# Order of the attention units in the first layer: short units one by one between long ones

## The reference, cut to what matters

```python
k_all = concatenate([k_ctx, k_lat], axis=1)         # 256 context + 1024 latent tokens
v_all = concatenate([v_ctx, v_lat], axis=1)
o_lat = _attend(q_block, k_all, v_all)              # per block of 128 latent queries
if with_ctx_out:                                    # first layer only
    o_ctx = _attend(heads_q(bq_c), k_ctx, v_ctx)    # context queries see 256 keys

def _attend(q, k, v):
    s = einsum('bqkgd,bskd->bkgqs', q, k) * ATTN_SCALE
    p = softmax(s, axis=-1)
    return einsum('bkgqs,bskd->bqkgd', p, v)
```

## Time and profile before

| | us |
|---|---|
| median of 3 runs (4020.82 to 4025.8) | 4024.08 |
| profiled execution | 4020.44 |
| its span | 4018.6 |
| PE busy (share of the span) | 3839.8 (96%) |
| DVE busy | 1755.6 (44%) |
| ACT busy | 1408.8 (35%) |

### The profile page before, as it was taken

One profiled execution on the slowest core, in us unless ns is written; L12 is line 12 of the kernel. 1 busy time (PEld: TensorE's weight loads), 2 busy tenths in 40 slices (PEclk: granted clock), 3 DMA queues, 4 the chain that ended last, 5 costly groups with the idle time before them and its releaser, 6 DMA issues.

```text
span 4018.6 us, 44730 instructions
## 1 busy us (share of the span) xinstructions
PE 3839.8 (96%) x16064; PEld 2101.0 (52%) x16064; DVE 1755.6 (44%) x3695; ACT 1408.8 (35%) x3419; POOL 714.8 (18%) x904
## 2 busy tenths in 40 slices
PE   8999899999999899999999999999999999979995
PEld 3444466655444466655466666545666644433331
DVE  3543567345254466445365465202233311254445
ACT  3433556123233455224345444311233312121112
POOL 1021000032012000032043344102222100013331
PEclk9999899999999999999999999999999999989997
DMA  5101210022110232122101001101101110159997
GB/s 209 42 1 37 93 69 25 30 79 74 72 42 1 105 126 75 37 76 74 65 6 40 22 27 68 46 18 55 44 12 42 67 42 0 64 201 362 369 355 279
DMA packets 88744, 346.64 MB, mean 86 GB/s; under 512 B 21176, under 2 KB 53440, under 8 KB 69712
## 3 DMA queue, kind: packets, MB, share of 16 engines
q1 hardware_dynamic: 70096, 304.94, 20.4%
q0 software_dynamic: 18432, 38.85, 2.6%
HBM read 401.31 MB, written 37.83 MB: 109 GB/s over the span
## 4 chain that ended last, share of the span: by engine, by line
PE 89%; DVE 4%; ACT 2%; issue 2%; DMA 1%; SPq 0%; POOL 0%; DVEq 0%; POOLq 0%; ACTq 0%
PE psum L88 40%; PE psum L94 9%; PE psum L1609 6%; PE psum L3434 6%; PE psum L2065 5%; PE psum L947 4%; PE psum L924 4%; PE psum L3456 3%; PE psum L2315 3%; PE psum L2083 1%; PE psum L320 1%; PE psum L2272 1%; PE psum L1446 1%; DMA arena<-w_in 0%; PE psum L1996 0%
## 5 line engine op out<-in xcount | busy, mean ns | idle before, releaser
L88 PE MATMUL psum<-arena 128*128 128x512 f32 (+3 forms) x4416 | 1737.4, 551 | 13.7 <-DVEq L180 8.1
L88 PEld LDWEIGHTS psum<-arena 128*128 128x128 f32 x4416 | 832.6, 191 | 835.0 <-issue 774.5
L94 PE MATMUL psum<-arena 128*128 128x128 f32 (+2 forms) x3020 | 437.5, 278 | 25.8 <-DMA arena<-hn_scratch,arena 5.8
L94 PEld LDWEIGHTS psum<-arena 128*128 128x128 f32 (+2 forms) x3020 | 340.5, 141 | 225.5 <-issue 158.3
L2065 PE MATMUL psum<-arena 128*128 128x512 f32 (+1 forms) x640 | 285.4, 573 | 9.0 <-DVE arena L2116 4.8
L1609 PE MATMUL psum<-arena 128*128 128x512 f32 x576 | 259.8, 599 | 0.9 <-ACT arena L1733 0.9
L3434 PE MATMUL psum<-arena 128*64 x512 | 229.0, 601 | 7.4 <-issue 5.7
L3435 PE MATMUL psum<-arena 128*64 128x512 f32 x512 | 229.0, 601 | 0.0
L947 PE MATMUL psum<-arena 64*128 64x512 f32 (+1 forms) x800 | 167.7, 551 | 21.3 <-ACT arena L1037 13.4
L1037 ACT ACTIVATE arena<-psum,arena 128x1280 f32<-128x1280 f32 (+1 forms) x144 | 176.8, 1233 | 20.0 <-DVE arena L989 18.2
L175 DVE SCALAR_TENSOR_TENSOR arena<-psum,arena 128x512 f32<-128x512 f32 x62 | 42.7, 689 | 299.3 <-ACT arena L172 299.3
(11 more groups left out here) (415 smaller groups left out, 4935.2 us busy)
## 6 DMA issues: line engine op xcount, KB each, us to landing
arena<-w_gu SPq DMA_DIRECT2D x32, 2048.0 KB, 10.4
arena<-w_ada SPq DMA_DIRECT2D x24, 2048.0 KB, 8.0
arena<-w_dn SPq DMA_DIRECT2D x32, 1024.0 KB, 14.7
arena<-w_in SPq DMA_DIRECT2D x12, 2048.0 KB, 8.7
arena<-w_out SPq DMA_DIRECT2D x6, 2048.0 KB, 8.1
arena<-gate_rows_scratch SPq DMA_DIRECT2D x36, 256.0 KB, 3.5
x_scratch<-arena SPq DMA_DIRECT2D x18, 512.0 KB, 3.2
arena<-x SPq DMA_DIRECT2D x16, 512.0 KB, 9.4
```

What stands on the lines that cost most here:

```text
L88: ins = e.matmul(out, l, r, start=(i == 0), stop=(i == n - 1))
L94: ins = e.transpose(o, i, idn)
```

## The change

The order of the units of the first layer. The second layer has no short units, so its order stays. The functions of the engines are not touched: they read the order from `att_units`.

```diff
         def att_units(l):
-            return [(t, h) for t in tiles_of(l) for h in range(0, 8, 2)]
+            short = [(t, h) for t in tiles_of(l) for h in range(0, 8, 2) if t < NC_T]
+            long = [(t, h) for t in tiles_of(l) for h in range(0, 8, 2) if t >= NC_T]
+            n = len(short) + len(long)
+            return [short.pop(0) if u % 4 == 1 and short else long.pop(0) for u in range(n)]
```

## The result

The changed kernel takes 4032.95 us (median of 7 runs, 4028.57 to 4036.91), the kernel before 4020.82 in the same number of runs (4008.9 to 4025.8). The ratio is 1.0036, 95% interval 1.0026 to 1.0045: slower by 12 us in the medians and 14 by the ratio. The profiled execution took 4033.37 us, its span is 4031.6, against 4018.6.

A forecast was written before the change was run, and what follows sets the result against it. PE's own work was taken to bound the long part, with the chain from scores to next scores just under it. To 4020.4 us came 14.6 for the order and 5 for clock falls: 4040.0 us, range 4026 to 4060.

The forecast's parts named there:

- the clock term: In the stage's slots with idle: three falls of PE's clock, 5 us; bounds 0 to 27 us.
- slots D: Slots with all neighbours long: 7.66 us as before, all PE work.
- Slot A: Slot with the short unit's scores, transposes and values of two long ones: all work, 5.95 us.
- B: Slot with long scores, the short unit's transposes and a product: 1.79 us idle, 9.27 us long.
- C: Slot with long scores, the short unit's values and the turn: some 1.7 us idle, 7.84 us long.
- Both gates: After long scores: product or turn not before 7.41 us, behind ACT's copy; next scores not before a 7.11 us chain.
- The start 14.2 us: Stage's first two slots: slot 0, long with nothing beside it, 8.5 us; slot 1, 5.7 us.
- The sum, +14.6 us to the scores of unit 39: Stage up to unit 39's scores: 299.9 us against 285.35 before, without any effect of the clock.
- my two kinds of row: PE idle of 3.15 us, or 0.66 and 1.13 close together, preceded clock falls; gaps such as 0.65 us didn't.
- The rival of falls in most rounds: Clock falls twelve times or more in the stage: 35 us, 4055, up to 4062 with sixteen; chance 0.14.
- The rival on the faster side: Short units' waits hidden, rounds pure PE work of 27.2 us: 13.6 us less, 4006.8; chance 0.12.
- The rival of no change: Gates come about 0.9 us sooner in 16 slots beside short units, 14.6 us in all: 4020; chance 0.08.

The follow-up runs named there:

- early_copy: Changed kernel with ACT's copy of the values of unit u-2 moved ahead of one or both exponentials where possible; 4022.46 us, ratio to before 1.0010.
- short_at_3: Changed kernel with the short units moved to slots 3, 7, ..., 31, the slots of the turns; ratio to before 1.0035.
- half: Changed kernel with four short units first (0 to 3) and the other four at slots 5, 9, 13 and 17; ratio to before 1.0017.
- short_last: Changed kernel with all 32 long units first and the 8 short ones at the end; 4011.31 us, ratio to before 0.9984.
- one_first: Against the kernel with all short units last: one short unit first, then 32 long, then the other 7 short; ratio to before 0.9974.
- short_last_2: The same kernel with all 8 short units last, run on a second occasion; ratio to before 0.9972.

## Why the prediction was right, and where it was off

The direction, the mechanism and the range held (4032.95 in 4026 to 4060); the point, 4040.0, was 7 us high. Had the clock term been left out, the sum would have been 4035.0, 2 us from the measured median; that is in part luck, since the stage came out 0.8 us longer than its sum and the time outside it 2 to 3 us shorter. Its steps:

- *PE's own work bounds the long part.* Held: slots D are 7.66 us in every kernel.
- *Slot A 5.95, B 9.27, C 7.84, D 7.66.* Measured 5.94, 9.24, 7.97, 7.66; a round 30.81 instead of 30.72. C came out 0.13 us long, 1 us over eight rounds, and the mis-sized term is the turn. Its gate came at 7.38 us as forecast (7.41), opened by ACT's copy, but from there to the next scores it took 0.59 us, not 0.43. The 0.43 of the earlier trace rows is what four transposes add behind others; four that stand alone take 0.58.
- *Both gates.* Shown: ACT's order by early_copy, the chain to the next scores by short_at_3. DVE's bank as the gate inside slot C is read from the wait (9.7 us, eight times) and from early_copy, where the slot lost only 0.25 us though ACT's copy had gone ahead; a kernel with another bank there was not run.
- *The start 14.2 us.* Measured 14.27 for slots 0 and 1 (410.63 to 424.90), partly at half clock, as in the earlier trace rows.
- *The sum, +14.6 us to the scores of unit 39.* Measured 300.76 - 285.32 = +15.4. One reading beside it was too low: the two slots behind the short units, 16.59 us, held about 4 us of idle, but by the pieces their work is only 3.74 + 5.79 = 9.5 us, so 7 us were idle or half-clock time. The sum doesn't use this number.
- *Three falls of the clock, 5 us.* This is the term that failed: none. I took slot B's idle to lie between the gaps that left the clock alone and those that made it fall, and expected three falls. With 1.7 to 2.1 us as the trace counts it, in eight slots here and four of half, none did. The nearer of my two kinds of row was a poor guide: the fall behind 0.66 and 1.13 us did not come in the changed kernel, with the same pieces. What makes the difference these runs don't show. The stage even has less half-clock time than before: by the mean clocks some 10 us (0.65 over the first two slots) against some 21 (0.79 over 32.86 + 16.59 us), an estimate; the gap of 3.15 us behind the eight short units is gone. The rival of falls in most rounds is refuted by the clock of 1.00. By it this kernel's trace disagrees with the Trainium skill's section on psum-queue depth-cycling ("TensorE: Matmul & The Clock Gate") as I had applied it: short stops between groups alone didn't make the clock go back and forth.
- *The rival on the faster side.* It needed the product's gate under 5.62 us; the product started at 7.38 in all eight. The rival of no change needed the gates about 0.9 us sooner; they came where they were before.
- *The medians.* I took the profiled execution and its 4020.44 as the base. Time outside the stage moved by several us with the clock, in both directions, so one profiled pair (+13.0) and the medians (+12.1) agree with the stage's +15.5 only within that.

## What to carry to other kernels

When a slot is the larger of one engine's work and a chain through the others, a small unit saves little in the slots where its work stands beside a big unit's chain (0.1 to 0.6 us a slot here): look for the slots u+1 and u+2 behind it, not for its own. Put units of one size together and let the order go from big to small, so that big work covers small chains. And before anything is put behind a wait "because the engine is idle there", read in which order the engine that must answer works: here one copy of 0.37 us stood behind 2.7 us of exponentials.

## What the runs showed of the hardware that was not expected

Idle pieces of 1.7 to 2.1 us ahead of a product, twelve of them in two kernels with PE at work on both sides, left the granted clock at 1.00; gaps of 3.15 and 3.16 us in two kernels were each followed by half clock.

The length of the gaps alone doesn't tell it. All eight profiles have the same two idle pieces at the stage's end (0.66 to 0.67 and 1.13 to 1.14 us), ahead of the same 32 products. In five (before, early_copy, half, short_at_3, short_last) a fall followed and the products took 9.29 us, in three (the changed kernel, one_first, short_last_2) none did and they took 7.60. Even the same kernel gave both, short_last first and short_last_2 second:

```profile
704.96 9.29 PE L88 MATMUL psum<-arena 128*128 128x272 f32 x32 [1.13 <-DVEq L180]
```
```profile
704.91 7.60 PE L88 MATMUL psum<-arena 128*128 128x272 f32 x32 [1.14 <-DVEq L180]
```

So whether such a place costs 1.7 us differs from run to run, and one profile of it, like the one in the earlier trace rows, is no measure. In the same two profiles the first two slots of the stage took 16.74 and 18.02 us; of these 1.28 us, 1.18 are PE's busy time (10.49 and 11.67 us), at clocks of 0.80 and 0.72.
